# Combine of each expert's output by row groups of the array, with accumulators laid out by quarters of the channels

## What is computed

```python
logits = (xf @ w_router + b_router).astype(jnp.float32)
top_val, top_idx = lax.top_k(logits, TOP_K)          # TOP_K = 4 of N_EXPERTS = 32
top_w = jax.nn.softmax(top_val, axis=-1)
...
def expert_chunk(args):
    toks, e = args
    hu = x_pad[toks] @ w_up[e] + b_up[e]             # w_up[e]: 1024 x 2048, float32
    return clamped_swiglu(hu) @ w_down[e] + b_down[e]  # w_down[e]: 1024 x 1024
...
out = jnp.zeros((n_tok + 1, d), jnp.float32).at[tok_buf].add(ys)[:n_tok]   # ys = output x gate
```

## Time and profile before

| | us |
|---|---|
| median of 3 runs (1434.57 to 1448.49) | 1434.88 |
| the profiled execution | 1438.32 |
| its span | 1436.5 |
| PE busy in it | 1272.6 |
| DMA: moved / mean rate | 463.78 MB / 323 GB/s |

### The profile page before, as it was taken

The page is one execution under the profiler, slowest core; times in us unless marked ns, Lnnn a source line. Parts: engine busy times, 40 slices in busy tenths (PEclk is TensorE's granted clock), DMA queues, the critical chain, the costliest instruction groups (busy, mean ns, idle before and its releaser), DMA issues.

```text
span 1436.5 us, 20931 instructions
## 1 busy us (share of the span) xinstructions
PE 1272.6 (89%) x8067; PEld 649.3 (45%) x8068; DVE 263.0 (18%) x736; ACT 294.6 (21%) x482; POOL 0.2 (0%) x4
## 2 busy tenths in 40 slices
PE   5999899998998999999788778877788899899996
PEld 2744688645344344345343443334334344534532
DVE  1123311215111121121112111111111112111212
ACT  2035422122212112112211112111112111100311
POOL 0000000000000000000000000000000000000000
PEclk8999999996999999999999999998999999899998
DMA  9943222595579999969999999999999999744880
GB/s 337 380 154 117 88 78 98 176 357 229 216 268 420 416 417 412 418 258 420 419 417 417 418 418 419 419 416 417 420 418 419 417 417 409 314 175 176 343 360 31
DMA packets 102073, 463.78 MB, mean 323 GB/s; under 512 B 8091, under 2 KB 9331, under 8 KB 69139
## 3 DMA queue, kind: packets, MB, share of 16 engines
q1 hardware_dynamic: 100368, 461.52, 80.3%
q10 hardware_dynamic: 1666, 1.72, 0.4%
HBM read 462.16 MB, written 1.05 MB: 322 GB/s over the span
## 4 chain that ended last, share of the span: by engine, by line
PE 62%; DMA 18%; SPq 13%; DVE 4%; issue 2%; ACT 1%; DVEq 0%
PE psum L519 17%; PE psum L857 17%; DMA ring<-in_w_up 14%; PE psum L935 10%; SPq L479 7%; PE psum L806 6%; PE psum L951 5%; SPq L474 5%; DMA ring<-in_w_down 3%; PE psum L849 2%; DMA ring<-in_ada_w 1%; PE psum L559 1%; DVE area L1501 1%; PE psum L525 1%; PE psum L899 1%
## 5 line engine op out<-in xcount | busy, mean ns | idle before, releaser
L857 PE MATMUL psum<-ring,area 128*32 128x512 f32 (+3 forms) x2496 | 401.5, 621 | 61.0 <-DMA ring<-in_w_up 61.0
L857 PEld LDWEIGHTS psum<-ring,area 128*32 128x32 f32 (+2 forms) x2496 | 103.1, 120 | 347.5 <-issue 230.3
L935 PE MATMUL psum<-ring,area 128*32 128x256 f32 (+1 forms) x2080 | 200.7, 422 | 28.0 <-DVE area L1493 15.5
L951 PE MATMUL psum<-area,hT 128*128 128x256 f32 (+1 forms) x512 | 137.7, 423 | 18.2 <-DVE area L1501 18.2
L806 PEld LDWEIGHTS psum<-area 128*128 128x128 f32 x1056 | 126.9, 200 | 34.1 <-issue 34.1
L935 PEld LDWEIGHTS psum<-ring,area 128*32 128x32 f32 (+1 forms) x2080 | 72.2, 115 | 146.3 <-issue 80.8
L806 PE MATMUL psum<-area 128*128 128x128 f32 x1056 | 133.4, 286 | 0.0
L951 PEld LDWEIGHTS psum<-area,hT 128*128 128x128 f32 x512 | 95.9, 192 | 62.7 <-DVE area L1501 35.2
L1121 ACT ACT_TABLE_LOAD x32 | 41.1, 1283 | 348.3 <-PE psum L832 348.3
L1130 ACT ACTIVATE area<-area 128x256 f32<-128x256 f32 (+1 forms) x52 | 21.5, 413 | 383.2 <-DVE area L1468 383.2
L1468 DVE TENSOR_SCALAR area<-psum 128x256 f32<-128x256 f32 (+1 forms) x52 | 21.8, 420 | 422.3 <-PE psum L857 422.1
(11 more groups left out here) (174 smaller groups left out, 667.5 us busy)
## 6 DMA issues: line engine op xcount, KB each, us to landing
ring<-in_w_up SPq DMA_DIRECT2D x256, 1024.0 KB, 19.1
ring<-in_w_down SPq DMA_DIRECT2D x128, 1024.0 KB, 22.6
ring<-in_ada_w SPq DMA_DIRECT2D x12, 2048.0 KB, 12.0
ring<-in_w_in SPq DMA_DIRECT2D x11, 2048.0 KB, 19.7
ring<-in_w_out SPq DMA_DIRECT2D x2, 2048.0 KB, 9.5
ring<-in_w_branch_b SPq DMA_DIRECT2D x1, 2048.0 KB, 7.4
cst<-in_cst ACTq DMA_DIRECT2D x1, 1168.0 KB, 8.0
x_res<-in_x SPq DMA_DIRECT2D x1, 1024.0 KB, 5.3
```

The lines of the kernel that those rows point to most:

```text
L857: ins = pe.matmul(ps[b][g * P // G:(g + 1) * P // G, 0:w], XT[:, kk, t0:t0 + P // G], wt[:, c0:c0 + w], start=False, stop=kk == KT - 1, sk ...
L935: ins = pe.matmul(ps[b][g * M:(g + 1) * M, 0:w], hidT[:, p, q * P + of * M:q * P + (of + 1) * M], down_weights(kk)[:, g * W + d * CW:g * W ...
L951: ins = pe.matmul(ps[2 * tt + c0 // CW][:, c0 % CW:c0 % CW + w], gates_, Y[:, p, c0 - g * W:c0 - g * W + w], start=False, stop=True, skip_ ...
```

## The change

The four accumulator banks now hold one quarter of the channels each, for both token tiles (`acc4`). The gates are turned into GT as they stand, with one ACT copy and without the zeroed copies in hT, and each matmul of the combine takes only the partition block r of GT and of Y, that is one group of 32 (or 64) rows of the array. Neighbouring matmuls use different row groups and write different banks. DVE's memset of hT and its semaphore are gone. The bias of the down projection (L785) is put into the banks in 8 matmuls of 256 columns in place of 4 of 512, and the final norm reads the banks in the new layout.

```diff
+        acc4 = psum[:, 0:4 * 512].rearrange("p (c t n) -> p c t n", c=4, t=TT)
...
-                pe.matmul(ps[b][:, :], gT[0:E, tt * P:(tt + 1) * P], b_down_sb[:, dh * 512:(dh + 1) * 512],
-                          start=True, stop=True, skip_group_check=True)
+                for tt in range(TT):
+                    pe.matmul(acc4[:, b, tt, :], gT[0:E, tt * P:(tt + 1) * P], b_down_sb[:, b * DQ:(b + 1) * DQ],
+                              start=tt == 0, stop=True, skip_group_check=True)
...
                 for p, (G, _) in enumerate(passes):
-                    W = D // G
-                    for g in range(G):
+                    for q in range(4 // G):
                         for tt in range(TT):
-                            gates_ = (GT[:, p, :] if G == 1 else GTg[G][:, g, :])[:, tt * P:(tt + 1) * P]
-                            for c0 in range(g * W, (g + 1) * W, min(W, CW)):
-                                w = min(W, CW)
-                                ins = pe.matmul(ps[2 * tt + c0 // CW][:, c0 % CW:c0 % CW + w], gates_,
-                                                Y[:, p, c0 - g * W:c0 - g * W + w],
-                                                start=False, stop=True, skip_group_check=True)
+                            for g in range(G):
+                                r = slice(g * P // G, (g + 1) * P // G)
+                                ins = pe.matmul(acc4[:, g * 4 // G + q, tt, :], GT[r, p, tt * P:(tt + 1) * P],
+                                                Y[r, p, q * DQ:(q + 1) * DQ], start=False, stop=True,
+                                                skip_group_check=True)
                 ins.then_inc(acc_done, 1)
...
-            act.wait_ge(gt_zero, 1)
...
-                for p, (G, _) in enumerate(passes):
-                    for g in range(G):
-                        r = slice(g * P // G, (g + 1) * P // G)
-                        ins = act.activation(GT[:, p, :] if G == 1 else GTg[G][r, g, :],
-                                             ps[7][r, p * T:(p + 1) * T], ACT.Copy)
-                ins.then_inc(gt_read, 1)
+                act.activation(GT[:, 0:len(passes), :],
+                               ps[7][:, 0:len(passes) * T].rearrange("p (c t) -> p c t", t=T), ACT.Copy).then_inc(gt_read, 1)
...
-                root_mean_square(psum[:, 2 * tt * 512:(2 * tt + 2) * 512], tt, 46, junk(tt))
+                root_mean_square(acc4[:, :, tt, :], tt, 46, junk(tt).rearrange("p (c n) -> p c n", c=4))
...
-            v.memset(hT[:, 0:6 * T], 0.0).then_inc(gt_zero, 1)
```

More of the change, by code:

```diff
@@ L48 @@
 CW = 512
+DQ = D // 4
 RING = 6
@@ L260, in layer_kernel @@
         GT = region(11264, (2, T))
-        GTg = {4: hT[:, 0:4 * T].rearrange("p (g t) -> p g t", g=4),
-               2: hT[:, 4 * T:6 * T].rearrange("p (g t) -> p g t", g=2)}
         xw = region(11776, (8, T))
@@ L311, in layer_kernel @@
         dn_tile = [sem(f"dn_tile{i}") for i in range(FT // 2)]
-        up_used, dn_used, gt_zero = sem("up_used"), sem("dn_used"), sem("gt_zero")
+        up_used, dn_used = sem("up_used"), sem("dn_used")
         xe_full, xe_read = sem("xe_full"), sem("xe_read")
@@ L782, in _ @@
             for b in range(4):
-                tt, dh = b // 2, b % 2
                 un.wait_free(pe, f"acc{b}")
-                pe.matmul(ps[b][:, :], gT[0:E, tt * P:(tt + 1) * P], b_down_sb[:, dh * 512:(dh + 1) * 512],
-                          start=True, stop=True, skip_group_check=True)
+                for tt in range(TT):
+                    pe.matmul(acc4[:, b, tt, :], gT[0:E, tt * P:(tt + 1) * P], b_down_sb[:, b * DQ:(b + 1) * DQ],
+                              start=tt == 0, stop=True, skip_group_check=True)
             for n in ("hb00", "hb01", "hb10", "hb11"):
@@ L1446, in _ @@
                     one_hot(0, k)
-            un.wait_full(v, "hb11")
-            v.memset(hT[:, 0:6 * T], 0.0).then_inc(gt_zero, 1)
             v.wait_ge(ld_small, 64)
@@ L1525, in _ @@
                     w = xn3[:, tt, dh * 512:(dh + 1) * 512]
-                    link(v.scalar_tensor_tensor(out=w, in0=ps[2 * tt + dh][:, :], scalar=small[:, 46 + tt:47 + tt],
-                                                in1=grow[:, dh * 512:(dh + 1) * 512], op0=ALU.mult, op1=ALU.mult))
+                    link(v.scalar_tensor_tensor(out=w.rearrange("p (c n) -> p c n", c=2),
+                                                in0=acc4[:, 2 * dh:2 * dh + 2, tt, :], scalar=small[:, 46 + tt:47 + tt],
+                                                in1=grow[:, dh * 512:(dh + 1) * 512].rearrange("p (c n) -> p c n", c=2),
+                                                op0=ALU.mult, op1=ALU.mult))
                     v.tensor_tensor(w, w, x3[:, tt, dh * 512:(dh + 1) * 512], ALU.add).then_inc(out_ready, 1)
```

## The result

| | before | change |
|---|---|---|
| first set, 4 runs each: median (lowest to highest) | 1434.73 (1434.57 to 1448.49) | 1419.13 (1415.49 to 1425.02) |
| ratio | | 0.988, interval 0.984 to 0.992 |
| change once more, beside 13 runs of before | 1441.7 (1434.29 to 1448.16) | 1415.21 (1412.59 to 1416.93) |
| ratio | | 0.982, interval 0.978 to 0.987 |
| span of the profiled execution | 1436.5 | 1423.1, then 1415.0 |

A forecast was written before the change was run, and what follows sets the result against it. Weight loads bound most of the expert loop; PE bounds the start, experts 3 to 7 and 25 to the end. Savings of 1.1 + 10.8 + 13.5 = 25.4 us take the median from 1434.88 to 1409.5; range 1403 to 1424.

The forecast's parts named there:

- case 1: Whole kernel: the forecast itself comes true, a gain of 22 to 29 us; chance 0.72.
- case 3: Whole kernel: gain partly given back (DMA rate, a moved instruction fetch, half the overlap), -5 to -14 us; chance 0.10.
- The combine itself: Combine matmuls overlap four or two at a time: k0 0.9 us, k1 1.7, k2 2.6, plus 0.1 for the first matmul.
- Rival 2: Combine: row groups do not run side by side in float32, all rows stay in line; 1434 to 1438 us; chance 0.12.
- The sequencer as the floor: Behind short combines PE's sequencer reaches the next stage late, 1.9 us after k0's start, 3.7 after k2's.
- Experts 3 to 7: Their combines, where PE is the limit: savings 1.4 + 3.3 + 1.6 + 1.2 + 3.3 = 10.8 us, if the loads allow it.
- expert 31's 4.2: Last expert's combine: ACT waits for the matmuls themselves, so 7.15 - 2.9 = 4.2 us are saved.
- only the queue's 1.1 us is won: Expert 0's combine: the sequencer is already the limit where a branch fetches its code, so the gain is 1.1 us.
- PE goes on to gathers without a branch: Expert 28's combine (k4): takes 4.6 us instead of 7.0, no branch following, a gain of 2.4 us.
- it wins nothing: Expert 27's combine: the jump to k4's body leaves PE idle for 4.38 us already, so no gain.
- The clock rival: Clock falls to 0.50 behind new idles after combines, 3.4 us per fall; no gain from 8 falls, 1450 with 12; chance 0.04.
- An end of the range: Expert 0's longer idle lowers the clock, expert 1's first tiles used up to 1.7 us later: total gain -22.

The follow-up runs named there:

- x_full_array: The change with row groups undone (zeroed gate copies, all 128 partitions, ACT's copies and DVE's memset of before), new layout kept: 1439.9 us, ratio 1.000.
- x_same_group: The change with the combine's loops turned, group outermost, so neighbouring matmuls use the same row group and bank: 1424.1 us, ratio 0.989.

## Why the prediction was right, and where its sum was off

- **The time**: in the range, in part by luck. The first set's -15.6 is a smaller gain than case 1's (-22 to -29) and just a larger one than case 3's (-5 to -14); the second set's -26.5 is in case 1. Case 3, at 0.10, had "an instruction fetch that moves" among its reasons, and fetches did move, beside the forecast's own mechanism. That the gain behind expert 27 made up for a part of the losses behind 0 and 28 was not foreseen.
- **What bounds the kernel**: right. The 19 combines under the loads gave nothing: the shift is -7.5 us at expert 10 and -7.3 at 25.
- **The combine itself**: right. 0.77 us between the first and last row's start in k0, four at a time, k1 1.62, k2 2.70; the nearest rows were the column groups', and they held. Rival 2 (no overlap) is out. With PE's code in almost the same place (`x_full_array`), the row groups are worth 24.7 us.
- **The sequencer as the floor**: right to 0.3 us. Forecast 1.9, 2.2, 2.35 and 3.7 us behind k0, k0 before k2, k1 and k2; measured 1.91, 2.16, 2.39, 3.97. k2's branch L432 came 1.95 us behind the combine's start rather than 1.6 (expert 0); that would fit a queue that takes a few instructions less than I had read, which no run tests.
- **Experts 3 to 7**: forecast 10.8, measured 9.9 and 9.8 (+2.4 to -7.5, +0.5 to -9.3).
- **The end**: expert 31's 4.2 came as 4.0 (-9.4 to -13.4; -17.5 to -21.5); ACT's first read is at 1410.10, 3.14 behind the combine's start, where 2.9 was forecast.

```profile
1410.10 1.02 ACT L976 ACTIVATE area<-psum 128x1024 f32<-128x1024 f32 x1 [15.69 <-PE psum L951]
```

- **The terms that failed** are three, and all took the sequencer's fetches as they stood in the trace of before. *Expert 0: "only the queue's 1.1 us is won"* became a loss of 3.1 and 3.5 us up to expert 3: two packets of instructions where one had been, and the clock at 0.50 behind an idle of 6.7 us (the price I had put at up to 1.7 us, as an end of the range). *Expert 28: 2.4 us, "PE goes on to gathers without a branch"* became a loss of 6.7 and 7.9: the branch stands behind the gathers, and two fetches of 3.7 and 4.9 us had come to it. *Expert 27: "it wins nothing"* became a gain of 3.9 and 9.7, as its fetch fell away (5.7 us; the rest is the clock behind it, at 0.50 for 10.2 us before, 13.7 in the first profile and 3.4 in the repeat). Together: forecast 3.5 us, measured -5.9 and -1.7. With 2.2 expected of experts 29 and 30 and 0.5 come in the first profile (2.2 in the repeat; a clock of 0.50 for 3.4 us at 1362 in the first), 0.9 of experts 3 to 7 and 0.7 to 3.0 us of gain ahead of the loop, this is the whole difference, to within 0.7 us, between 25.4 and 13.4 or 21.5 us of span.
- **The clock rival**: no fall came behind the short idles of 0.8 to 0.9 us between experts 3 and 8; falls came in the idles of 6.7 and 8.1 us. One more, of 3.4 us, starts at 1361.67 in the first profile, 2.6 us behind the start of expert 30's combine, and has no counterpart in the repeat; what set it is not shown.
- **The signs**: two that the prediction named went against it, "expert 27 as long as before" (8.10 to 2.39 us) and new falls of PEclk behind combines before 643 or after 1157 us (412.76, 1317.29, 1361.67). The first two falls come with the fetches, which the list of signs had left out.
- **An end of the range**: expert 0's clock alone takes 25.4 to 23.7; the -22 written beside it needs the overlap of only two as well.

## What to carry to other kernels

Row groups in neighbouring matmuls, with a bank for each, run side by side in float32 just as column groups do (whether the banks have to differ, no run here tests); but once the work behind which the loop's branches are hidden is cut from 3.6 to 1.1 us, the sequencer is what you wait for, so clear its path in the same edit. In a loop over several bodies, read the branches' own rows (a branch of 0.2 us that takes 3 to 6) before trusting a difference of 1%: shifting the same code by 128 instructions cost the kernel before 15.9 us, as much as the change gave in the first set, and every edit shifts code. Compare two versions at more than one placement.

## What the runs showed of the hardware that I had not expected

- Matmuls are, as I read the rows' spacing and lengths, not kept in the program's order across row groups: with two matmuls of each group written together, all four groups still started within 0.05 us of each other, every 0.22 us; with four together, the second group started 0.97 us late, past three rows of the first. The Trainium skill ("TensorE: Matmul & The Clock Gate", Part 3) has matmuls start strictly in order. By the rows of k1 in `x_same_group` that does not hold here: in strict order a row would start 6 ns behind one of its own group, where the others of that group start 0.216 us apart.
- A branch within which one packet of instructions starts took 3.3 to 4.1 us where no weights moved, and 5.9 to 6.2 us beside weights at 406 to 421 GB/s; with two packets it took 4.5 to 5.1 us where none moved. Behind expert 0, at 139 to 166 GB/s, it was 3.59 us in before with one packet and 5.85 and 4.81 in the change's two profiles with two.
- The clock ahead of the loop is at 0.50 for 17 us in some executions and for 3.4 us in others of the same program.
